# Seven norms of a transformer kernel: three of eight scaled input tiles made by GpSimd instead of VectorE

## Chip, cores and metric

One core of a Trainium2 chip runs the whole program. The metric is the device time of one execution in microseconds (us); of several runs the median is given. Engines: TensorE (PE in the rows, PEld its weight loads), VectorE (DVE), ScalarE (ACT), GpSimd (POOL) and SyncE (SP).

## What is computed

A sequence of 512 tokens, 1024 wide, goes through four layers. Layers 0 and 1 (`first_block`) each have a mixer and an MLP with a LayerNorm behind each; the input of the next matmul is the normed value scaled and shifted by a modulation of a condition vector:

```python
def layer_norm(x, g, b):
    mu = jnp.mean(xf, axis=-1, keepdims=True)
    var = jnp.mean(jnp.square(xf - mu), axis=-1, keepdims=True)
    return (xf - mu) * lax.rsqrt(var + LN_EPS) * g + b
...
x = layer_norm(ALPHA * x + gate * y, ln_g[layer, 0], ln_b[layer, 0])
u = x * (1.0 + scale) + shift          # input of the next matmuls
```

The two hybrid layers (`hybrid_layer`) have RMS norms, once before the mixer and once before the gated feed-forward:

```python
h = rms_norm_2(x, norm_mix) * (1 + sc_m) + sh_m
...
h = rms_norm_2(x, norm_ffn) * (1 + sc_f) + sh_f
```

All is float32.

## The kernel before

Activations lie transposed: 8 tiles of 128 features by 512 tokens each. `X` ("residual") is the residual stream, `H` ("hidden") 32 tiles of work space, `M` ("mixer_out") eight more, `TMP` ("tmp") two, `COL` ("columns") and `GAINS` small columns with one number per partition.

Each float32 matmul is done as three matmuls on rounded parts: a weight panel is split into a high part (ScalarE, line 2024) and a low part (VectorE, line 1275), an input tile likewise into `UHI` ("in_high") and `ULO` ("in_low"), and TensorE multiplies high x high, high x low and low x high. Weight panels stream in by SyncE's DMA queue through a ring of 4; three split panels are kept. `prepare(ahead(...))` places the splitting in each engine's instruction list, always the next panels, and each waits until an older panel has been used.

The work of each engine is an instruction list written out by hand, in program order, with semaphores between the lists: an event name (`mark`, `at`) stands for a semaphore and its value.

A norm, around the change, goes like this. TensorE forms the mean of squares in a bank. ScalarE makes the root (the reciprocal square root) of it, by Ln (line 2066) and Exp (line 2069), and marks it `ln_r` or `rms_r`. VectorE then runs `norm_split` (line 1420): for tile k a scaled tile, `X[k] * gain[k] * root`, written to `H[16 + k]` (line 1429); ScalarE adds the shift and rounds, which gives `UHI[k]` (line 2129, `norm_high`); VectorE forms the low half, `H[16 + k] + shift - UHI[k]`, in `ULO[k]` (line 1424, `tile_low`). VectorE's order is scaled 0, scaled 1, low 0, scaled 2, low 1, and so on, scaled 7, low 6, low 7. TensorE meanwhile runs filler matmuls (`busy`, line 625).

There are seven such norms: `("ln", 0)`, `("ln", 1)`, `("ln", 2)` in the first block (called norm 0, 1 and 2), and `("mix", l)` and `("ffn", l)` for l = 0, 1 in the hybrid layers. They start at about 244.6, 607.0, 952.4, 1324.4, 1695.5, 2062.7 and 2428.6 us (norm 0, 1, 2, mix 0, ffn 0, mix 1, ffn 1). The norm behind the last MLP of the first block and the final one have no such split.

Behind six of them TensorE runs `gemm_pair` (lines 697 to 699): two panels at once on two banks, the second two tiles behind the first, so that a tile brings three matmuls for tiles 0 and 1 and six from tile 2 on; it waits for `norm_out` of each tile. Behind norm 1 it runs a single `gemm` (lines 654 to 656), with three matmuls per tile, and then `gemm_tok` (lines 715 to 717).

In the LayerNorms `layer_norm` (line 1383) first centres the eight tiles of X (line 1392), then makes the columns `LNG` (gain) and `LNS` (shift, lines 1396 to 1399, marked `ln_shift`), and then waits for the root. In mix 0 the tiles of X are finished by line 1413 (`ln_x`). In the others of the hybrid layers they are finished by the residual's additions (line 1336, `x_new`).

GpSimd's list is short: `gpsimd_program` stores rows of the forget gate to memory (line 2630) and loads 16 rows broadcast over the partitions (line 2635), each from the fifth on behind a wait on the attention.

Of the kernel before, what the change touches and what calls it, by code (L numbers as in the profile page):

```python
# [9 lines left out]
KT = D // P  # L10
# [18 lines left out]
L2 = 2  # L29
FF2 = 2816  # L30
FF2_T = FF2 // P
HALF = 16
# [274 lines left out]
class Ledger:  # L307
# [11 lines left out]
    def step(self, name, by=1):  # L319

        sem = self.sem(name)
        self.value[name] += by
        return sem, by

    def mark(self, name, *event, by=1):

        sem = self.sem(name)
        self.value[name] += by
        self.also(name, *event)
        return sem, by  # L330
# [6 lines left out]
    def last(self, name):  # L337

        return self.sem(name), self.value[name]

    def at(self, *event):

        if not self.table:
            return self.sem("unknown"), 1
        name, value = self.table[event]
        return self.sem(name), value


def build(nc, io, table):
    ev = Ledger(nc, table)  # L350
    at, mark, step, last = ev.at, ev.mark, ev.step, ev.last
    v, s, g, pe, sp = nc.vector, nc.scalar, nc.gpsimd, nc.tensor, nc.sync
# [6 lines left out]
    def sb(name, shape, dt=F32):  # L359
        return nc.alloc_sbuf_tensor(name, shape, dt)  # L360
# [5 lines left out]
    X = sb("residual", [P, KT, T])  # L366
# [5 lines left out]
    H = sb("hidden", [P, 32, T])  # L372
# [32 lines left out]
    R = TMP[:, 0, 0:T]  # L405
# [5 lines left out]
    ln_root = lambda i: M[:, 7, :] if i in (0, 2) else R  # L411
    LNG, LNS, RB = (COL[:, 88 + 8 * z:96 + 8 * z] for z in range(3))
# [9 lines left out]
    mix = lambda k: M[:, k, :]  # L422
    u_split = lambda k: (UHI[:, k, :], ULO[:, k, :])
    h_split = lambda k: (HSPLIT[:, 0, k, :], HSPLIT[:, 1, k, :])
    STAGE = 16
    landed = [nc.alloc_semaphore(f"panel_landed_{k}") for k in range(RING)]
    stage_mod = lambda n: MODS[:, 24 * n:24 * n + 24]

# [56 lines left out]
    mix_gain = lambda l: GAINS[:, 16 * l:16 * l + 8]  # L485
    ffn_gain = lambda l: GAINS[:, 16 * l + 8:16 * l + 16]
# [781 lines left out]
    def vector_program():  # L1268
# [114 lines left out]
        def layer_norm(i, gcol_, bcol, mod):  # L1383
# [20 lines left out]
            if mod is not None:  # L1404
                norm_split(("ln", i), lambda k: LNG[:, k:k + 1], lambda k: LNS[:, k:k + 1], ln_root(i))
# [14 lines left out]
        def norm_split(event, gain, shift, root, ready=None):  # L1420

            def tile_low(k):
                v.wait_ge(*at("norm_high", *event, k))
                v.scalar_tensor_tensor(ULO[:, k, :], H[:, STAGE + k, :], shift(k), UHI[:, k, :].bitcast(F32), ALU.add,  # L1424
                                       ALU.subtract).then_inc(*mark("vector_norm", "norm_out", *event, k))
            for k in range(KT):
                if ready is not None:
                    v.wait_ge(*at(*ready, k))
                v.scalar_tensor_tensor(H[:, STAGE + k, :], X[:, k, :], gain(k), root, ALU.mult, ALU.mult).then_inc(
                    *mark("vector_norm", "norm_scaled", *event, k))  # L1430
                if k:
                    tile_low(k - 1)
            tile_low(KT - 1)

        def rms_norm(event, gain, shift):
            v.wait_ge(*at("rms_r", *event))
            norm_split(event, lambda k: gain[:, k:k + 1], lambda k: shift[:, k:k + 1], R,
                       ("ln_x", 3) if event == ("mix", 0) else None)

        def input_low(k, src, high, event):  # L1440
            v.wait_ge(*at(*high))
            v.tensor_tensor(ULO[:, k, :], src, UHI[:, k, :].bitcast(F32), ALU.subtract).then_inc(
                *mark("vector_norm", *event))
# [543 lines left out]
        for n in range(4):  # L1987
            for k in (2 * n, 2 * n + 1):
                prepare(ada_panels[k + 8] + 1)
                v.wait_ge(*at("x", n))  # L1990
                v.wait_ge(*last("modulations"))
                v.tensor_scalar(H[:, STAGE + k, :], X[:, k, :], MODS[:, 8 + k:9 + k], MODS[:, k:k + 1], ALU.mult,
                                ALU.add).then_inc(*mark("vector_start", "u_stage", k))
            prepare(PANELS[("xr", n)][0] + 1)
            for k in (2 * n, 2 * n + 1):
                input_low(k, H[:, STAGE + k, :], ("u_high", k), ("u_low", k))
        even()
# [17 lines left out]
    def scalar_program():  # L2015
# [31 lines left out]
        def input_high(k, src, ready, event):  # L2047
            s.wait_ge(*at(*ready))
            s.activation(UHI[:, k, :], src, ACT.Copy).then_inc(*mark("scalar_norm", *event))
# [76 lines left out]
        def norm_high(event, shift):  # L2126
            for k in range(KT):
                s.wait_ge(*at("norm_scaled", *event, k))
                s.activation(UHI[:, k, :], H[:, STAGE + k, :], ACT.Identity, bias=shift[:, k:k + 1]).then_inc(
                    *mark("scalar_norm", "norm_high", *event, k))  # L2130
# [461 lines left out]
        for n in range(4):  # L2592
            prepare(PANELS[("xr", n)][0] + 1)
            for k in (2 * n, 2 * n + 1):
                input_high(k, H[:, STAGE + k, :], ("u_stage", k), ("u_high", k))
        s.wait_ge(*at("loads"))
# [29 lines left out]


    def gpsimd_program():
        g.wait_ge(*at("forget"))
        g.dma_start(io["forget"], NF).then_inc(*mark("forget_stored", "forget_stored", by=16))  # L2630
        g.wait_ge(*at("forget_stored"))
        for hd in range(FOX_H):
            if hd >= 4:
                g.wait_ge(*at("fox", "max", 8 * ((hd - 4) // 2) + 6 + hd % 2))
            g.dma_start(fox_bias(hd), io["forget"][hd:hd + 1, :].broadcast_to([P, T])).then_inc(
                *mark(f"bias_landed_{hd % 4}", "bias_landed", hd, by=16))


    def sync_program():
# [19 lines left out]
    vector_program()  # L2659
    scalar_program()  # L2660
    gpsimd_program()
    sync_program()
    return ev.made
# [32 lines left out]
```

## Time and profile before

| | us |
|---|---|
| median of 3 runs | 2809.56 |
| lowest and highest run | 2802.15, 2810.24 |
| the profiled execution, its own time | 2805.29 |
| its span | 2803.7 |
| TensorE busy | 2681.7 (96%) |
| VectorE busy | 1626.8 (58%) |
| ScalarE busy | 1153.0 (41%) |
| GpSimd busy | 9.4 (0%) |
| granted TensorE clock, mean | 0.995 |

The span is the time from the first to the last recorded instruction of one profiled execution; all rows come from it. Busy times of TensorE are of pipelined matmuls with modelled ends. "Waits" are idle times of an engine just before an instruction, put down to the instruction that released it. [...]

### The profile page before, as it was taken

Reading aid. Unit: us, or ns where it says so; the run is one execution under the profiler, and the core shown is the slowest. Engines: PE = TensorE matmul, PEld = TensorE weight load, DVE = VectorE, ACT = ScalarE, POOL = GpSimd, SP = SyncE. Lnnn points to the kernel's source line nnn. Section 1 sums busy time; section 2 is a strip of 40 time slices with the busy share of each in tenths; the row PEclk is TensorE's granted clock in tenths of the full one; section 3 lists DMA queues with packets and bytes.
Section 4 is the critical chain, followed back from the end, with each engine's and each line's share of the span. In section 5 each row is a group of like instructions: output and inputs, shape, how many; then the busy total and the mean of one; then the engine's idle time right before and its main releaser. Section 6 shows DMA issues by size and latency. Waiting matters only on the chain.

```text
span 2803.7 us, 41785 instructions
## 1 busy us (share of the span) xinstructions
PE 2681.7 (96%) x17242; PEld 2116.3 (75%) x17242; DVE 1626.8 (58%) x2917; ACT 1153.0 (41%) x2012; POOL 9.4 (0%) x21
## 2 busy tenths in 40 slices
PE   6999999999999999999998899999999988999998
PEld 4777888867666788886886667888878766788886
DVE  6588746573556874667556665444465577533334
ACT  2544324234556442323645553221355466322222
POOL 0000000000000000000000000000000000000000
PEclk9999999999999999999999999999999999999999
DMA  6445555533221365553230013444443200222222
GB/s 256 137 135 181 187 187 177 183 118 107 82 68 54 106 203 201 187 203 130 98 128 17 3 54 121 135 150 143 137 136 107 97 3 3 92 96 98 98 98 83
DMA packets 92093, 336.42 MB, mean 120 GB/s; under 512 B 10480, under 2 KB 10736, under 8 KB 91776
## 3 DMA queue, kind: packets, MB, share of 16 engines
q1 hardware_dynamic: 86800, 315.40, 33.7%
q10 hardware_dynamic: 3792, 14.11, 1.4%
q0 software_dynamic: 1312, 4.23, 0.5%
q8 instruction: 138, 2.26, 0.3%
q14 instruction: 51, 0.42, 0.0%
HBM read 331.57 MB, written 2.13 MB: 119 GB/s over the span
## 4 chain that ended last, share of the span: by engine, by line
PE 46%; ACT 4%; DVE 3%; issue 1%; DVEq 0%; ACTq 0%
PE bank L654 12%; PE bank L655 12%; PE bank L656 12%; PE bank L936 1%; ACT probs L2269 1%; PE bank L921 1%; PE bank L907 1%; PE bank L1008 1%; PE bank L697 0%; PE bank L699 0%; PE bank L698 0%; PE bank L1170 0%; PE bank L996 0%; PE bank L1180 0%; PE bank L1118 0%
## 5 line engine op out<-in xcount | busy, mean ns | idle before, releaser
L1275 DVE TENSOR_TENSOR weights_low<-weight_ring,weights_high 128x1024 fp32r<-128x1024 f32 x404 | 493.8, 1224 | 423.2 <-ACT weights_high L2024 423.0
L654 PE MATMUL bank<-in_high,weights_high 128*128 128x512 f32 x1848 | 725.6, 393 | 9.6 <-DVE in_low L1424 3.4
L655 PE MATMUL bank<-in_low,weights_high 128*128 128x512 f32 x1848 | 720.0, 390 | 0.0
L656 PE MATMUL bank<-in_high,weights_low 128*128 128x512 f32 x1848 | 719.9, 390 | 0.0
L2024 ACT ACTIVATE weights_high<-weight_ring 128x1024 fp32r<-128x1024 f32 x404 | 424.5, 1051 | 419.7 <-PE bank L656 302.2
L654 PEld LDWEIGHTS bank<-in_high,weights_high 128*128 128x128 f32 x1848 | 347.2, 188 | 90.7 <-issue 5.4
L656 PEld LDWEIGHTS bank<-in_high,weights_low 128*128 128x128 f32 x1848 | 347.3, 188 | 72.9
L655 PEld LDWEIGHTS bank<-in_low,weights_high 128*128 128x128 f32 x1848 | 347.3, 188 | 71.0 <-issue 0.5
L654 PE MATMUL bank<-hidden_split,weights_high 128*128 128x512 f32 x864 | 336.9, 390 | 0.0
L656 PE MATMUL bank<-hidden_split,weights_low 128*128 128x512 f32 x864 | 336.1, 389 | 0.0
L655 PE MATMUL bank<-hidden_split,weights_high 128*128 128x512 f32 x864 | 336.1, 389 | 0.0
L1284 DVE CUSTOM_DVE_ANT_0 weight_ring<-weight_ring,silu_c,vectors 128x1024 f32<-128x1024 f32 x192 | 244.4, 1278 | 3.7 <-DMA weight_ring<-stream 3.6
L654 PEld LDWEIGHTS bank<-hidden_split,weights_high 128*128 128x128 f32 x864 | 162.2, 188 | 34.2 <-issue 0.5
L655 PEld LDWEIGHTS bank<-hidden_split,weights_high 128*128 128x128 f32 x864 | 162.2, 188 | 34.0 <-issue 0.5
L656 PEld LDWEIGHTS bank<-hidden_split,weights_low 128*128 128x128 f32 x864 | 162.2, 188 | 33.7
L2139 ACT ACTIVATE hidden_split<-tmp 128x512 fp32r<-128x512 f32 x108 | 68.3, 632 | 269.3 <-DVE tmp L1811 200.8
L2038 ACT ACTIVATE tmp<-bank 128x512 f32<-128x512 f32 (+1 forms) x69 | 41.2, 598 | 219.5 <-PE bank L656 219.0
L1447 DVE TENSOR_TENSOR hidden_split<-tmp,hidden_split 128x512 fp32r<-128x512 f32 x108 | 74.8, 692 | 75.4 <-ACT hidden_split L2139 75.4
L1336 DVE SCALAR_TENSOR_TENSOR residual<-bank,modulations,residual 128x512 f32<-128x512 f32 x64 | 48.0, 750 | 118.7 <-PE bank L656 118.7
L2269 ACT ACTIVATE probs<-probs,columns 128x256 f32<-128x256 f32 (+4 forms) x144 | 73.7, 513 | 102.1 <-DVE columns L1618 100.3
L2038 ACT ACTIVATE tmp<-bank,vectors 128x512 f32<-128x512 f32 (+1 forms) x65 | 44.7, 687 | 129.0 <-PE bank L656 125.8
L1811 DVE TENSOR_TENSOR tmp<-bank,tmp 128x512 f32<-128x512 f32 x44 | 30.4, 692 | 113.6 <-PE bank L656 113.6
(385 smaller groups left out, 3334.9 us busy)
## 6 DMA issues: line engine op xcount, KB each, us to landing
weight_ring<-stream SPq DMA_DIRECT2D x597, 512.0 KB, 3.4
mixer_out<-cmp ACTq DMA_DIRECT2D x6, 1024.0 KB, 5.3
hidden<-forget_rows POOLq DMA_DIRECT2D x16, 256.0 KB, 3.6
residual<-x ACTq DMA_DIRECT2D x4, 512.0 KB, 12.4
mixer_out<-cmp SPq DMA_DIRECT2D x2, 1024.0 KB, 6.3
out<-mixer_out ACTq DMA_DIRECT2D x4, 512.0 KB, 2.7
constants<-consts ACTq DMA_DIRECT2D x1, 1821.5 KB, 20.5
silu_c<-c ACTq DMA_DIRECT2D x2, 512.0 KB, 4.2
```

Source lines behind the costliest of these rows:

```text
L654: pe.matmul(bank[:, :], WHI[:, z, cols], high, start=(k == 0), stop=False)
L655: pe.matmul(bank[:, :], WHI[:, z, cols], low, start=False, stop=False)
L656: ins = pe.matmul(bank[:, :], WLO[:, z, cols], high, start=False, stop=(k == ktiles - 1))
L1275: v.tensor_tensor(WLO[:, z, :], ring[:, n % RING, :], WHI[:, z, :].bitcast(F32), ALU.subtract).then_inc(*mark("weights_low", "low", n))
L1284: v.tensor_tensor_reduce(w, w, SC[:, :], 1.0, vec1("ada_b", col, col + 1), ALU.mult, ALU.add, MODS[:, col:col + 1]).then_inc(*mark("modula ...
L1336: v.scalar_tensor_tensor(X[:, m, :], B_of(key)[:, :], gcol_[:, m:m + 1], X[:, m, :], ALU.mult, ALU.add).then_inc(*mark("residual", "evicte ...
L1447: v.tensor_tensor(HSPLIT[:, 1, at_, :], tmp, HSPLIT[:, 0, at_, :].bitcast(F32), ALU.subtract).then_inc(*mark("vector_mlp", *event))
L1811: v.tensor_tensor(tmp, B_of(("gup", l, j))[:, :], tmp, ALU.mult).then_inc(*mark("vector_mlp", "evicted", ("gup", l, j)))
L2024: s.activation(WHI[:, i % NSPLIT, :], ring[:, n % RING, :], ACT.Copy).then_inc(*mark("weights_high", "high", n))
L2038: s.activation(dst, view(B_of(key)[:, :]), func, **kw).then_inc(*mark("scalar_evict", "evicted", key))
L2139: s.activation(HSPLIT[:, 0, at_, :], tmp, ACT.Copy).then_inc(*mark("scalar_mlp", *event))
L2269: s.activation(p, p, ACT.Exp, bias=nm, scale=-1.0, accum_out=COL[:, c + 2 + z:c + 3 + z]).then_inc(*mark(sem, *name, "exp", i))
```

## The change

VectorE's `norm_split` makes scaled tiles 0 to 4 only. GpSimd makes tiles 5, 6 and 7 in two operations each: X times the gain column, as soon as the tile of X and the gain are there, and, once the root is there, that times the root, in place in `H[16 + k]`. It marks the same event as VectorE did, so ScalarE's `norm_high` waits for it. All eight low halves stay with VectorE. GpSimd's list gets norms 0 and 1 ahead of the forget store, norm 2 behind the bias loads, and then the four norms of the hybrid layers.

```diff
+    POOL_TILES = 5
...
             for k in range(KT):
-                if ready is not None:
-                    v.wait_ge(*at(*ready, k))
-                v.scalar_tensor_tensor(H[:, STAGE + k, :], X[:, k, :], gain(k), root, ALU.mult, ALU.mult).then_inc(
-                    *mark("vector_norm", "norm_scaled", *event, k))
+                if k < POOL_TILES:
+                    if ready is not None:
+                        v.wait_ge(*at(*ready, k))
+                    v.scalar_tensor_tensor(H[:, STAGE + k, :], X[:, k, :], gain(k), root, ALU.mult, ALU.mult).then_inc(
+                        *mark("vector_norm", "norm_scaled", *event, k))
                 if k:
                     tile_low(k - 1)
...
     def gpsimd_program():
+
+        def norm_tiles(event, gain, root, centred, ready):
+            for k in range(POOL_TILES, KT):
+                g.wait_ge(*at(*centred(k)))
+                g.tensor_scalar(H[:, STAGE + k, :], X[:, k, :], gain(k), None, ALU.mult).then_inc(*step("gpsimd_norm"))
+            g.wait_ge(*at(*ready))
+            g.wait_ge(*last("gpsimd_norm"))
+            for k in range(POOL_TILES, KT):
+                g.tensor_tensor(H[:, STAGE + k, :], H[:, STAGE + k, :], root, ALU.mult).then_inc(
+                    *mark("gpsimd_norm", "norm_scaled", *event, k))
+
+        def layer_tiles(i):
+            g.wait_ge(*at("ln_shift", i))
+            norm_tiles(("ln", i), lambda k: LNG[:, k:k + 1], ln_root(i), lambda k: ("ln_centre", i, k), ("ln_r", i))
+
+        layer_tiles(0)
+        layer_tiles(1)
         g.wait_ge(*at("forget"))
...
+        layer_tiles(2)
+        for l in range(L2):
+            g.wait_ge(*at("gains", l, 1))
+            norm_tiles(("mix", l), lambda k: mix_gain(l)[:, k:k + 1], R,
+                       lambda k: ("x_new", "ffn", l - 1, HALF, KT - 1) if l else ("ln_x", 3, k), ("rms_r", "mix", l))
+            g.wait_ge(*at("gains", l, 4))
+            norm_tiles(("ffn", l), lambda k: ffn_gain(l)[:, k:k + 1], R, lambda k: ("x_new", "hyb", l, KT - 1), ("rms_r", "ffn", l))
```

## Rows read from the trace of the kernel before

**Rows 1.** The page: busy time of each engine, and the chain that ended last.
```profile
PE 2681.7 (96%) x17242; PEld 2116.3 (75%) x17242; DVE 1626.8 (58%) x2917; ACT 1153.0 (41%) x2012; POOL 9.4 (0%) x21
...
PE 46%; ACT 4%; DVE 3%; issue 1%; DVEq 0%; ACTq 0%
```
**Rows 2.** TensorE's waits: line waited for, us in total, times, longest us.
```profile
PE bank L697 <- DVE in_low L1424: 8.9, 18, 1.0
...
PE bank L654 <- DVE in_low L1424: 3.4, 7, 1.3
```
**Rows 3.** VectorE's timeline, norm ffn 0: start us, us, engine line op, [idle before].
```profile
1695.50 1.42 DVE L1429 SCALAR_TENSOR_TENSOR hidden<-residual,gains_of_layer,tmp 128x512 f32<-128x512 f32 x2 [3.39 <-ACT tmp L2069]
1697.04 0.75 DVE L1424 SCALAR_TENSOR_TENSOR in_low<-hidden,modulations,in_high 128x512 fp32r<-128x512 f32 x1
...
1701.02 0.75 DVE L1424 SCALAR_TENSOR_TENSOR in_low<-hidden,modulations,in_high 128x512 fp32r<-128x512 f32 x1
1701.68 0.75 DVE L1429 SCALAR_TENSOR_TENSOR hidden<-residual,gains_of_layer,tmp 128x512 f32<-128x512 f32 x1
...
1706.83 1.23 DVE L1275 TENSOR_TENSOR weights_low<-weight_ring,weights_high 128x1024 fp32r<-128x1024 f32 x1 [0.20 <-ACT weights_high L2024]
```
**Rows 4.** TensorE's timeline, the same norm: the first matmul of each tile's three.
```profile
1697.93 0.47 PE L697 MATMUL bank<-in_high,weights_high 128*128 128x512 f32 x1 [0.76 <-DVE in_low L1424]
...
1699.17 0.50 PE L697 MATMUL bank<-in_high,weights_high 128*128 128x512 f32 x1 [0.30 <-DVE in_low L1424]
...
1700.49 0.50 PE L697 MATMUL bank<-in_high,weights_high 128*128 128x512 f32 x1 [0.36 <-DVE in_low L1424]
...
1701.99 0.40 PE L697 MATMUL bank<-in_high,weights_high 128*128 128x512 f32 x1
...
1706.11 0.39 PE L697 MATMUL bank<-in_high,weights_high 128*128 128x512 f32 x1
...
1707.47 0.39 PE L697 MATMUL bank<-in_high,weights_high 128*128 128x512 f32 x1
```
**Rows 5.** TensorE's timeline, norm 1: the first and the last tile.
```profile
609.46 0.47 PE L654 MATMUL bank<-in_high,weights_high 128*128 128x512 f32 x1 [1.35 <-DVE in_low L1424]
...
618.20 0.50 PE L654 MATMUL bank<-in_high,weights_high 128*128 128x512 f32 x1
```
**Rows 6.** ScalarE's timeline, norm ffn 0: the root, and the high half of tile 5.
```profile
1694.77 0.63 ACT L2069 ACTIVATE tmp<-tmp 128x512 f32<-128x512 f32 x1
...
1702.46 0.72 ACT L2129 ACTIVATE in_high<-hidden,modulations 128x512 fp32r<-128x512 f32 x1 [0.60 <-DVE hidden L1429]
```
**Rows 7.** GpSimd's timeline: its forget store.
```profile
629.85 0.62 POOL L2630 DMA_DIRECT2D forget_rows<-hidden  x1 [629.41 <-DVE columns L1660]
```
**Rows 8.** Groups of VectorE by line and shape: count | busy us, mean ns | idle before.
```profile
L1275 DVE TENSOR_TENSOR weights_low<-weight_ring,weights_high 128x1024 fp32r<-128x1024 f32 x404 | 493.8, 1224 | 423.2 <-ACT weights_high L2024 423.0
...
L1457 DVE TENSOR_TENSOR tmp<-tmp 128x512 f32<-128x512 f32 x64 | 44.3, 692 | 53.2 <-ACT tmp L2038 53.0
...
L1413 DVE TENSOR_SCALAR residual<-residual,vectors 128x512 f32<-128x512 f32 x8 | 3.3, 487 | 0.0
```
**Rows 9.** VectorE's timeline where norm 0, norm 1 and mix 0 begin.
```profile
244.57 1.42 DVE L1429 SCALAR_TENSOR_TENSOR hidden<-residual,columns,mixer_out 128x512 f32<-128x512 f32 x2 [4.71 <-issue]
...
606.76 0.16 DVE L1400 TENSOR_SCALAR columns<-vectors 128x8 f32<-128x8 f32 x1
606.96 1.41 DVE L1429 SCALAR_TENSOR_TENSOR hidden<-residual,columns,tmp 128x512 f32<-128x512 f32 x2
...
1324.42 1.42 DVE L1429 SCALAR_TENSOR_TENSOR hidden<-residual,gains_of_layer,tmp 128x512 f32<-128x512 f32 x2 [1.80 <-ACT tmp L2069]
```
**Rows 10.** Stretches: A:B, us, busy of PE, PEld, DVE, ACT, POOL (count), granted clock, DMA.
```profile
1507.40:1514.20 6.80, 4.76 (x124) 3.56 (x116) 5.89 (x18) 4.20 (x17) 0.00 (x0) 1.00 0.01 4
1514.20:1521.00 6.80, 6.19 (x86) 4.64 (x88) 5.31 (x18) 3.91 (x16) 0.00 (x0) 0.50 0.01 4
...
1695.50:1701.00 5.50, 4.08 (x14) 2.10 (x13) 5.37 (x8) 2.83 (x4) 0.00 (x0) 1.00 0.01 3
```

## The prediction

> **What bounds the kernel now.** I read the page first, for the share of each engine and the chain: TensorE is busy 2681.7 of 2803.7 us, VectorE 1626.8, and the chain that ended last runs mostly over the weight matmuls [rows 1]. So a microsecond counts only where it makes TensorE wait, and a VectorE microsecond saved elsewhere is worth nothing. Next I read who waits for the line that the norms end in, the low half L1424: TensorE lost 8.9 us in 18 waits at the paired matmuls and 3.4 us in 7 at the single ones [rows 2]. That is 12.3 us for all seven norms. A change over about 8.4 us (0.3%, about what a measurement of this kernel can tell from no change) would need two thirds of it back.
>
> Third, the timelines of one norm on three engines, the first ffn norm, at 1695.5 us; the other five paired norms have the same pattern, to about 0.1 us. VectorE waits 3.39 us for the root, then issues scaled and low operations in turn with starts 0.66 us apart, so one tile each 1.32 us [rows 3]. TensorE starts tiles 0, 1 and 2 at 1697.93, 1699.17 and 1700.49, each after a wait on VectorE, and then waits no more: tile 3 starts at 1701.99 and tile 7 at 1707.47, so a tile on two banks takes 1.37 us, its three matmuls 0.69 on one [rows 4]. The 18 waits are thus these three in each of six norms. VectorE at 1.32 feeds TensorE at 1.37, with no reserve to speak of: tile 3's low half ends at 1701.77 (1701.02 + 0.75) for matmuls at 1701.99. The norm's whole time for TensorE is decided by how early the first three tiles come; whatever holds VectorE by 1 us in them holds TensorE by nearly 1 us to the end.
>
> Fourth, the one norm with single matmuls (index 1, 607 us). There a tile takes TensorE 0.69 us, so it waits on each up to tile 6; the first is at 609.46, the last at 618.20 [rows 5]. VectorE is the bound over the whole norm, and only here are tiles 5 to 7 on the path.
>
> **The change part by part.** *Removed from VectorE:* three scaled operations in each of seven norms, 21 at a step of 0.66 us, 13.9 us in all. In the six paired norms they lie behind tile 2, where TensorE does not wait, so they are worth 0 there; the cover is the 1.37 us of matmuls per tile. VectorE's next work behind a norm is the low half of a panel, already waiting for ScalarE's high half (0.20 us idle before it in [rows 3]), which waits for a panel to be used: finishing the norm earlier brings it no earlier. In norm 1, tiles 5, 6 and 7 could go at ScalarE's 0.72 us [rows 6] in place of 1.32: 3 x 0.60 = 1.8 us gained, if GpSimd is in time.
>
> *Added on GpSimd:* per norm three multiplications by the gain (one tensor input) and three by the root (two). The trace has no such operation; GpSimd is busy 9.4 us in all, with 16 bias loads, one store and four tiny fills [rows 1]. Bounds for the product with the root, 128x512 with two inputs: 0.69 us, VectorE's tensor_tensor of that size, and 1.22, its tensor_tensor of twice the size [rows 8]. I take 1.22, because a norm gets no shorter by erring low and the engine has never been seen doing such work here. For the multiplication by the gain: 0.49 us (VectorE's one-input operation) to 1.22; I take 0.69. [...]
>
> *Is GpSimd in time?* In the ffn norm its products would end 1.22, 2.44 and 3.66 us behind the root at 1695.4, by 1699.1 (by about 1701 if each first waits for a VectorE operation); ScalarE turns to tile 5 at 1702.46 [rows 6]. VectorE idles 3.39 us ahead of the root in the ffn norms and in mix 1, 4.71 in norm 0, 1.80 in mix 0 [rows 3, 9]: there the gain multiplications hide (3 x 0.69 = 2.1 us; in mix 0 they can start behind the last additions to X, about 0.8 us ahead of the pause). In norms 1 and 2 the shift columns come only 0.2 us before VectorE's own first tile (606.76 against 606.96 in [rows 9]), so the gain multiplications run beside VectorE. Even there six operations end within 5.8 us, before tile 5 is due. GpSimd's queue: norms 0 and 1 are placed ahead of the forget store at 629.85 [rows 7], which they clear by 13 us; norm 2 stands behind the bias loads, which are long over by then. Nothing queued is late.
>
> *Unknown: what GpSimd's operations do to VectorE beside them.* Every VectorE operation of the norm reads two tiles from SBUF (hidden and in_high, residual and root) and writes a third [rows 3]. From below the cost is 0: the engines run side by side. From above it is the whole duration of each GpSimd operation: while one runs, the other stands. I take the upper end, as the operands of both are the same kind and the same tiles. [...]
>
> Then, per norm, taking turns: three products of 1.22 put 3.66 us between VectorE's first operations: behind scaled 0, behind scaled 1, behind low 0. TensorE's tile 2 comes 3.66 us later, and later tiles keep their distance. Norms 0, mix 0, mix 1, ffn 0, ffn 1: 5 x 3.66 = 18.3 us. Norm 2 adds 3 x 0.69 = 2.1 us of gain multiplications: 5.7. Norm 1: 5.7 less the 1.8 gained: 3.9. Sum 18.3 + 5.7 + 3.9 = 28 us slower. With the low prices (0.69 and 0.49): 5 x 2.07 + 3.54 + 1.74 = 15.6.
>
> *The clock.* [...] Such a stretch costs up to 3.4 us of matmul time; I allow half of it for each norm, 12 us, and put it into the upper end, not the sum, since TensorE would be waiting for VectorE in part of it.
>
> **The rivals.** *A, taking turns* (the forecast): +28 us on the profiled execution's 2805.3 us (span 2803.7 and 1.6 around it), so 2833. The median of the runs, 2809.6, lies 4.3 us above that execution and their lowest, 2802.2, 3 below; I leave the sum where the profile puts it. For it: both engines read the same two kinds of tiles out of the same memory in the same 5 us, and VectorE has no pause in which three products would fit before tile 3. Own range 2818 to 2848. Chance 0.63.
> *B, side by side* (not slower): VectorE's 0.75 us stay 0.75 beside GpSimd. Nothing changes in six norms, norm 1 gains 1.8: 2803.5. It decides as long as GpSimd's product stays under about 3.4 us (tile 7's matmuls start at 1707.47 in [rows 4]; its low and high half take 0.75 and 0.72, so the third product must end by about 1705.8, 10.4 us behind the root). For it: the tiles are late in order. [...] Chance 0.22.
> *C, VectorE keeps its turn:* its operations overlap by 0.08 us, so GpSimd may get in only where VectorE pauses. The first long pause would be behind low 3, at 1701.77, as low 4 now waits for ScalarE. Then the three products run to about 1706.9 in turn with low 4 and 5, low 6 ends about 1707.7 instead of in time for 1706.1: 1.7 us per paired norm, with norm 1 about level: +10, 2815. Chance 0.12.
> *D, clearly faster:* only the 3.4 us at single matmuls can shrink by moving late tiles [rows 2], so 8.4 us is beyond the mechanism; 0.03 is left for what I do not see.
>
> **Numbers.** Forecast 2833. The range 2804 to 2848 reaches from B's edge to A with dear products and some clock lost. Slower by over 0.3%: A and two thirds of C, 0.71; faster 0.04 (D, noise on B); same 0.25.
>
> **What would show it.** Under A: scaled and low operations of tiles 0 to 2 keep near 0.75 us in length or grow to about 2, but their starts spread by 1.2 us, TensorE's waits on L1424 grow from 12.3 to about 40 us, and L1429 counts 35 instead of 56. Under B: starts 0.66 us apart as before, with GpSimd's rows beside them. Under C: GpSimd's first product starts or ends about 6 us behind the root. The forecast is wrong if tile 2's matmuls start at the same distance from the root as now (5.1 us), or if GpSimd's product takes over 2 us, when A would near 2850.

## The result and the profile after

The changed kernel takes 2837.8 us, the median of 4 runs (2835.6 to 2839.1), against 2806.8 of the kernel before (4 runs, 2802.2 to 2810.2). The ratio is 1.0112 with a 95% interval of 1.0097 to 1.0126: 31 us slower. The profiled execution took 2839.1 us (span 2837.6), 33.8 above the one of before.

VectorE first, the same norm as in [rows 3] (ffn 0), timeline of the changed kernel (start, length, engine, line; the scaled tiles are now line 1431, the low halves 1425):

```profile
1711.08 1.75 DVE L1431 SCALAR_TENSOR_TENSOR hidden<-residual,gains_of_layer,tmp 128x512 f32<-128x512 f32 x2 [3.39 <-ACT tmp L2071]
1712.96 1.54 DVE L1425 SCALAR_TENSOR_TENSOR in_low<-hidden,modulations,in_high 128x512 fp32r<-128x512 f32 x1
1714.43 1.77 DVE L1431 SCALAR_TENSOR_TENSOR hidden<-residual,gains_of_layer,tmp 128x512 f32<-128x512 f32 x1
1716.12 1.75 DVE L1425 SCALAR_TENSOR_TENSOR in_low<-hidden,modulations,in_high 128x512 fp32r<-128x512 f32 x1
1717.80 0.74 DVE L1431 SCALAR_TENSOR_TENSOR hidden<-residual,gains_of_layer,tmp 128x512 f32<-128x512 f32 x1
```

GpSimd beside it (timeline; the three operations of the first line are those with the gain, of the second those with the root). Over all norms a product with the root shows as 1.3 to 1.8 us, most often as 1.7:

```profile
1707.87 4.64 POOL L2635 TENSOR_SCALAR hidden<-residual,gains_of_layer 128x512 f32<-128x512 f32 x3 [362.39 <-DVE residual L1337]
1712.65 4.67 POOL L2639 TENSOR_TENSOR hidden<-hidden,tmp 128x512 f32<-128x512 f32 x3
```

Three VectorE operations are 0.8 to 1.0 us longer than 0.75 us, and they are the three beside GpSimd's three products (1712.65 to 1717.3). The moment GpSimd is done, VectorE is back at 0.74 us. The first pair, 1.75 us in place of 1.42, runs beside the tail of the third gain product (1710.94 to 1712.51).

TensorE in the same norm. Tiles 0, 1, 2 and 7 start 3.67, 6.95, 8.39 and 16.01 us behind the root (at 1710.98), where [rows 4] has 2.53, 3.77, 5.09 and 12.07 behind 1695.40:

```profile
1714.65 0.47 PE L698 MATMUL bank<-in_high,weights_high 128*128 128x512 f32 x1 [1.89 <-DVE in_low L1425]
...
1717.93 0.79 PE L698 MATMUL bank<-in_high,weights_high 128*128 128x512 f32 x1 [2.34 <-DVE in_low L1425]
1718.52 0.63 PE L699 MATMUL bank<-in_low,weights_high 128*128 128x512 f32 x1
...
1719.37 0.67 PE L698 MATMUL bank<-in_high,weights_high 128*128 128x512 f32 x1
...
1726.99 0.39 PE L698 MATMUL bank<-in_high,weights_high 128*128 128x512 f32 x1
```

From tile 1 until 1720.9 its matmuls take 0.63 us in place of 0.40 and come 0.43 us apart in place of 0.23. The stretches say why (columns as in [rows 10], the clock is the third number from the end, 1.00 being full speed):

```profile
1711.00:1717.50 6.50, 2.69 (x9) 1.24 (x7) 6.29 (x5) 2.11 (x3) 6.17 (x4) 1.00 0.01 3
1717.50:1721.00 3.50, 3.07 (x7) 2.31 (x8) 3.37 (x6) 1.83 (x3) 0.00 (x0) 0.51 0.00 0
```

TensorE stood for more than half of 6.5 us, and then had 0.51 of its clock, that is, nearly all of the second stretch at half speed (0.50 over 1717.60 to 1720.90). Each of the seven norms has such a half-speed stretch in this profile, 3.4 us long in three and 6.8 in four, 37.5 us together; the kernel before has none in a norm.

Over the program, TensorE's waits on the low halves grew from the 12.3 us of [rows 2] to 29.9:

```profile
PE bank L698 <- DVE in_low L1425: 24.2, 16, 2.5
...
PE bank L655 <- DVE in_low L1425: 5.7, 5, 2.4
```

And VectorE, with 21 operations fewer, is busier: 1636.5 us against 1626.8, GpSimd 78.3 against 9.4:

```profile
PE 2696.7 (95%) x17242; PEld 2128.3 (75%) x17242; DVE 1636.5 (58%) x2896; ACT 1151.1 (41%) x2012; POOL 78.3 (3%) x63
```

Where do the 33.8 us of this profile arise? Fillers aside, both traces hold the same 17096 matmuls in the same order, so the start of each can be set against its start before. Take a norm as the stretch from 2.5 us ahead of VectorE's first scaled tile to 22 us behind it, in the time of the kernel before. TensorE then loses 5.1, 1.7, 4.0, 4.6, 3.9, 6.0 and 4.1 us in the seven norms, 29.4 in all: it stands 16.5 us longer, and is busy 12.9 us longer with the same matmuls. Ahead of the first norm it is 2.8 us late already, and the parts between and behind the norms make the rest.

### The profile page after: what moved, and what is told of

It is laid out like the page before. It is cut to its first block, busy times and chain, and to the rows that moved or that the text cites. A ratio compares the mean times of both kernels' runs of the same rounds, so it can differ in the third digit from the quotient of the medians.

```text
span 2837.6 us, 41822 instructions
## 1 busy us (share of the span) xinstructions
PE 2696.7 (95%) x17242; PEld 2128.3 (75%) x17242; DVE 1636.5 (58%) x2896; ACT 1151.1 (41%) x2012; POOL 78.3 (3%) x63
## 3 DMA queue, kind: packets, MB, share of 16 engines
q1 hardware_dynamic: 86800, 315.40, 33.8%
## 4 chain that ended last, share of the span: by engine, by line
PE 45%; DVE 4%; ACT 4%; issue 1%; DVEq 0%; ACTq 0%
PE bank L655 12%; PE bank L656 12%; PE bank L657 12%; ACT probs L2271 1%; PE bank L937 1%; PE bank L922 1%; PE bank L698 1%; PE bank L1009 1%; PE bank L908 1%; DVE hidden L1431 0%; PE bank L699 0%; PE bank L700 0%; DVE in_low L1425 0%; PE bank L1171 0%; PE bank L997 0%
## 6 DMA issues: line engine op xcount, KB each, us to landing
residual<-x ACTq DMA_DIRECT2D x4, 512.0 KB, 12.3
```

## The experiments

The theories. *Turns*: a GpSimd operation that reads SBUF keeps a VectorE operation with two SBUF inputs waiting, whatever data they work on. *Late tiles*: the cost comes from waiting for GpSimd's scaled tiles. Beside turns, *the clock*: part of the cost is TensorE's half-speed stretches that the longer stops set off.

**1. GpSimd's operations without anyone waiting for them.** VectorE makes all eight tiles as before; GpSimd works on constants and a scratch tile at the same moments.

```diff
+    SCR = sb("scratch", [P, T])
...
+        def extra(which):
+            for _ in range(3):
+                if ev.value.get("gpsimd_extra"):
+                    g.wait_ge(*last("gpsimd_extra"))
+                if which == 0:
+                    ins = g.tensor_scalar(SCR[:, :], const("cos"), vec1("final", 0, 1), None, ALU.mult)
+                else:
+                    ins = g.tensor_tensor(SCR[:, :], SCR[:, :], const("sin"), ALU.mult)
+                ins.then_inc(*step("gpsimd_extra"))
+
+        def norm_tiles(centred, ready):
+            g.wait_ge(*at(*centred))
+            extra(0)
+            g.wait_ge(*at(*ready))
+            extra(1)
```

> The kernel before, all eight scaled tiles by VectorE, plus six GpSimd operations in each of the seven norms at the times of the change (three one-input products, then three two-input products behind the root). They read constants and write a scratch tile that nobody reads, so no engine waits for them. Taking turns: each GpSimd operation that runs beside VectorE makes one VectorE operation about 1.0 us longer (as 0.75 became 1.75 us), so this costs at least what the change did, about 30 us (25 to 40). Rival, late tiles (the cost comes from waiting for GpSimd's scaled tiles): within 3 us of before, and VectorE's operations keep 0.75 us.

Measured: ratio 1.0108 (1.0093 to 1.0123), 30 us slower (28 by the medians), as much as the change. VectorE's timeline of ffn 0 in this kernel, with GpSimd's products at 1711.62 to 1716.30:

```profile
1711.72 1.77 DVE L1430 SCALAR_TENSOR_TENSOR hidden<-residual,gains_of_layer,tmp 128x512 f32<-128x512 f32 x1
1713.41 1.75 DVE L1425 SCALAR_TENSOR_TENSOR in_low<-hidden,modulations,in_high 128x512 fp32r<-128x512 f32 x1
...
1716.76 0.74 DVE L1425 SCALAR_TENSOR_TENSOR in_low<-hidden,modulations,in_high 128x512 fp32r<-128x512 f32 x1
```

No engine waits for a GpSimd result here, so late tiles falls as the cause. The cost is the mere presence of GpSimd's operations. It is also as large with VectorE's 21 scaled operations back in place: in the six paired norms TensorE loses 28.0 us here and 27.7 in the changed kernel, so taking them away brought nothing there.

**2. GpSimd writing only.** As 1, with six fills of the scratch tile in place of each three operations.

```diff
-            for _ in range(3):
+            for _ in range(6):
...
-                    ins = g.tensor_scalar(SCR[:, :], const("cos"), vec1("final", 0, 1), None, ALU.mult)
+                    ins = g.memset(SCR[:, :], 0.0)
...
-                    ins = g.tensor_tensor(SCR[:, :], SCR[:, :], const("sin"), ALU.mult)
+                    ins = g.memset(SCR[:, :], 0.0)
```

> The kernel before plus twelve GpSimd fills of the scratch tile (128x512) in each norm, six ahead of the root and six behind: operations that write SBUF and read nothing. If the two engines take turns only over reading, VectorE's operations keep 0.75 us and the time is within 3 us of before. If they take turns over any SBUF access, VectorE's operations beside the fills grow and the time is 15 us or more above before. Late tiles: within 3 us of before.

Measured: 1.0003 (0.9993 to 1.0012), no difference. The groups of GpSimd by line (us busy, mean ns), and VectorE's timeline where six of the fills run from 1696.30 to 1699.74:

```profile
L2638 POOL MEMSET scratch<- 128x512 f32 x42 | 22.0, 525 | 4.0 <-ACT mixer_out L2070 1.3
```
```profile
1697.58 0.75 DVE L1425 SCALAR_TENSOR_TENSOR in_low<-hidden,modulations,in_high 128x512 fp32r<-128x512 f32 x1
```

VectorE keeps 0.74 to 0.75 us beside the fills. GpSimd's fills, which only write, did not hold it; the products of run 1, which also read, held it to 1.75 to 1.77.

**3. VectorE reading one tile from SBUF and one from PSUM.** As 1, but three two-input products beside the centring of X (X minus a bank) in the four LayerNorms, and nothing in the norms.

```diff
+        def extra(i):
+            g.wait_ge(*(at("ln_mean", i) if i else at("ln_mean", i, KT - 1)))
+            for _ in range(3):
...
+                g.tensor_tensor(SCR[:, :], SCR[:, :] if _ else const("cos"), const("sin"), ALU.mult).then_inc(*step("gpsimd_extra"))
```

> The kernel before plus three GpSimd two-input products on constants and a scratch tile beside the centring of X in each of the four LayerNorms, where VectorE reads one tile from SBUF and one from PSUM. If turns are taken only against VectorE operations with two SBUF inputs, the centring keeps 0.68 us and the time stays within 3 us of before. If GpSimd's reading holds every VectorE operation, some centrings grow to about 1.7 us and the four norms are later by up to 3 us each, 12 us in all.

Measured: 1.0001 (0.9992 to 1.001). VectorE's and GpSimd's timelines at norm 1:

```profile
602.55 1.88 DVE L1393 TENSOR_TENSOR residual<-residual,bank 128x512 f32<-128x512 f32 x3 [2.25 <-issue]
```
```profile
602.90 2.63 POOL L2636 TENSOR_TENSOR scratch<-scratch,constants 128x512 f32<-128x512 f32 x2
```

The centrings keep 0.68 us each (three in 1.88, overlapped; 0.67 to 0.69 for all 32 of the four norms), and GpSimd's products go at 1.3 us in place of 1.7. With one operand in PSUM the two engines ran side by side. Runs 1 to 3 together: operations of VectorE with two SBUF inputs were held (0.75 us became 1.75), and that only beside GpSimd operations that read SBUF. The hold is not the length that the profile shows for the GpSimd operation: VectorE lost 1.0 us to a product that shows as 1.3 us where it need not wait (run 6), and 0.43 to a gain operation of at least 1.56 us (run 5).

**4. The products with the root later.**

```diff
             g.wait_ge(*last("gpsimd_norm"))
+            g.wait_ge(*at("norm_out", *event, 2))
             for k in range(POOL_TILES, KT):
```

> The changed kernel, with GpSimd's three products with the root started only when VectorE has the low half of tile 2. Taking turns: the first three tiles are no longer held by products, and the holds fall where tiles 5 to 7 give VectorE 2 us back, so about 12 us above before (8 to 20) instead of 31. Rival, late tiles: tiles 5 to 7 come about 5 us later still, so clearly more than 31 us above before.

Measured: 1.0054 (1.0037 to 1.0071), 15 us slower than before and half of the change's 31, although tiles 5 to 7 come later. VectorE is held as much as in the changed kernel, but in the low halves of tiles 3 to 7, five in 6.50 us (3.61 in the changed kernel), behind GpSimd's products at 1707.93:

```profile
1708.34 6.50 DVE L1425 SCALAR_TENSOR_TENSOR in_low<-hidden,modulations,in_high 128x512 fp32r<-128x512 f32 x5
```

TensorE's waits on the low halves are 19.2 us here, and it loses 14.1 us in the norms. Two things make up the saving. With the shorter stops only norms 1 and 2 keep a half-speed stretch, 10.2 us together in place of 37.5. And the holds themselves count for less: in the five paired norms without such a stretch TensorE loses 1.9 us each, where it loses 3.2 when the holds fall on the first tiles at full clock (run 10). So when VectorE is held counts, and not only for how long in total.

**5. The gain on GpSimd, the root on VectorE.**

```diff
+                else:
+                    v.wait_ge(*at("norm_gained", *event, k))
+                    v.tensor_tensor(H[:, STAGE + k, :], H[:, STAGE + k, :], root, ALU.mult).then_inc(
+                        *mark("vector_norm", "norm_scaled", *event, k))
...
-            for k in range(POOL_TILES, KT):
-                g.tensor_tensor(H[:, STAGE + k, :], H[:, STAGE + k, :], root, ALU.mult).then_inc(
-                    *mark("gpsimd_norm", "norm_scaled", *event, k))
```

> The changed kernel with GpSimd doing only the three one-input products with the gain; VectorE does the products with the root for tiles 5 to 7 (16 operations a norm, as before). Taking turns: only the gain products that run on behind the root cost, three in norms 1 and 2, one or two in the others: 9 to 14 us above before. Rival, only the two-input products collide (my sum let the gain products hide in five norms and took 0.69 us for each): under 6 us above before.

Measured: 1.0016 (1.0006 to 1.0025), 4 to 5 us (1.7 to 7), below what I expected of turns and inside the rival's number. But the trace shows that gain products do hold VectorE, only for 0.43 us each (norm 1, VectorE's timeline; 0.74 without a hold):

```profile
611.10 1.17 DVE L1425 SCALAR_TENSOR_TENSOR in_low<-hidden,columns,in_high 128x512 fp32r<-128x512 f32 x1
```

I had priced the one-input operation's hold at the product's 1.0 us. In this profile, 6.4 us above the one of before, TensorE loses 2.3 us in the norms and the rest elsewhere. So of the 31 us some 2 to 5 are the gain's; the rest needs the products.

**6. Only tile 7 on GpSimd.**

```diff
-    POOL_TILES = 5
+    POOL_TILES = 7
```

> The changed kernel with only tile 7 made by GpSimd. Taking turns, one two-input product per norm behind the root holds VectorE 1.0 us, the gain product 0.4 in norms 1 and 2 and nothing elsewhere, less 0.6 gained in norm 1: about 7 us above before, and no half-speed stretch if one shorter stop does not tip the clock. If cost went with the number of tiles alone, clock included, it would be a third of 31, 10 us. Late tiles: 0, since tile 7 alone is in time by far.

Measured: 1.0032 (1.0019 to 1.0045), 9 us (5 to 13). Seven holds of 1.03 us (ffn 0: the two first scaled operations take 2.45 us in place of 1.42) give 7.2. The interval takes in 7 and 10, so the time does not tell a third of everything from the holds alone. The trace does: ffn 0, mix 1 and ffn 1 cost TensorE 1.0 us each, just the hold, and norm 1 0.4. The expectation of no half-speed stretch was wrong: norm 0, norm 2 and mix 0 have one of 3.4 us, and cost 1.95, 1.95 and 1.7. Late tiles' 0 is excluded again. VectorE's and GpSimd's timelines in ffn 0:

```profile
1701.79 2.45 DVE L1431 SCALAR_TENSOR_TENSOR hidden<-residual,gains_of_layer,tmp 128x512 f32<-128x512 f32 x2 [3.39 <-ACT tmp L2071]
```
```profile
1701.77 1.26 POOL L2639 TENSOR_TENSOR hidden<-hidden,tmp 128x512 f32<-128x512 f32 x1 [1.63 <-ACT tmp L2071]
```

The single product is 1.26 us long and holds VectorE 1.03. Where three follow one another, starts of held VectorE operations are 1.69 us apart (1714.43 and 1716.12 in the changed kernel), VectorE's own step of 0.66 and the hold of 1.03. The 1.7 us that the profile shows for the later products take in that VectorE operation; they are no price of the product.

**7. and 8. The change again, and with fillers in TensorE's stops.** The changed kernel once more, unedited, beside one with more filler matmuls (the diff shows the mix pair; the up and the gate pairs are edited likewise):

> The changed kernel as it is, beside the two below on one chip: 1.0112 of before again, within its interval (1.0097 to 1.0126), and a half-speed stretch of TensorE's clock in each of the seven norms.

```diff
-        def gemm_pair(keys, x, ready, between=lambda k: None, idle=5):
+        def gemm_pair(keys, x, ready, between=lambda k: None, idle=5, fill={}):
...
                 between(k)
+                busy(banks[1], fill.get(k, 0))
...
-            gemm_pair(ropes[0:2], u_split, lambda k: ("norm_out", "mix", l, k))
+            gemm_pair(ropes[0:2], u_split, lambda k: ("norm_out", "mix", l, k), idle=8, fill=({1: 3, 2: 4}, {1: 6, 2: 3})[l])
```

> The changed kernel with more filler matmuls (128x384, about 0.33 us each) where TensorE stands in the six paired norms: ahead of tile 0 (8, 10 or 12 in place of 5 or 10) and between tiles 0 and 2 (3 to 9, on the second bank, which is not yet in use). VectorE's holds stay. If the granted clock costs its own part (my reading of the trace: about 10 of the 31 us), the half-speed stretches of these norms go and the time falls by 5 to 10 us against the changed kernel, to 21 to 26 us above before. If the clock costs nothing beside the waits, the time stays within 3 us of the changed kernel.

Measured: the change again 1.0099 (1.0085 to 1.0112), with a half-speed stretch in each of the seven norms as expected; with fillers 1.0093 (1.0077 to 1.0109). Inconclusive: the six paired norms had lost their half-speed stretches, but each filler is two recorded matmuls, 0.67 us and not the 0.33 that I had taken from a row counting both. TensorE's own queue of fillers had become the wait (in ffn 0 twelve recorded matmuls, 4.03 us, stand between tiles 0 and 1, and tile 1 starts behind them without a wait), so the run tells nothing of the clock's price.

**9. and 10. Fillers that fit.** The same with 6 to 11 ahead of tile 0 and 1 to 4 behind it, beside the changed kernel:

```diff
-            gemm_pair(ropes[0:2], u_split, lambda k: ("norm_out", "mix", l, k), idle=8, fill=({1: 3, 2: 4}, {1: 6, 2: 3})[l])
+            gemm_pair(ropes[0:2], u_split, lambda k: ("norm_out", "mix", l, k), idle=6, fill=({1: 1, 2: 2}, {1: 3, 2: 1})[l])
```

> The changed kernel as it is, beside the one below: 28 to 31 us above before.

> The changed kernel with fillers that fit the stops. In the run before, each filler was two recorded matmuls (0.67 us and not 0.33), so they overran the stops and held tiles 0 and 1 back themselves. Now 6, 7, 8 or 11 ahead of tile 0 and 1 to 4 between tiles 0 and 2. VectorE's holds stay. If the clock costs its own part, the half-speed stretches of the six paired norms go, and the time falls 5 to 10 us below the changed kernel beside it. If it costs nothing beside the waits, it stays within 3 us of it.

Measured: the changed kernel 2838.1 us (5 runs, 2832.8 to 2842.2; ratio 1.0107, 1.0091 to 1.0122), with fitting fillers 2830.6 (5 runs, 2828.6 to 2834.2; ratio 1.0087, 1.0074 to 1.01). The medians are 7.5 us apart; the intervals still touch, so that size is a likely one and not a sharp one. TensorE's tile 1 in ffn 0, behind fillers from 1711.68 to 1713.78, and the stretch around it:

```profile
1714.19 0.50 PE L699 MATMUL bank<-in_high,weights_high 128*128 128x512 f32 x1 [0.41 <-DVE in_low L1426]
```
```profile
1712.00:1719.00 7.00, 6.23 (x24) 4.14 (x23) 6.87 (x10) 4.29 (x7) 1.58 (x1) 1.00 0.00 0
```

Tile 1 starts as late behind VectorE as in the changed kernel (3.28 us behind tile 0 in both), but the clock stays at 1.00. Only norm 1, which got no fillers, keeps its half-speed stretch. Matmul by matmul, as above, TensorE loses 19.0 us in the six paired norms here, and 27.7, 28.5 and 26.9 in the three profiles of the changed kernel (the one taken beside this run has its stretch in six of the seven norms; norm 2 has none). So VectorE's holds at the first tiles cost about 19 us there, and the slower clock that the longer stops bring 8 to 9.5 more.

No kernel tried here beats the one before.

## Why the prediction was right

**The sign, the mechanism and the size** held: forecast 2833, measured 2838, rival A (taking turns). Run 1 shows the mechanism apart from everything else, and runs 2 and 3 show its conditions. B (side by side) fell with the first rows of the profile after; C (VectorE keeps its turn) too, since GpSimd's first product ends 3 us behind the root and not 6. D (clearly faster) did not come. Tile 2 starts 8.4 us behind the root and not 5.1, and no product takes 2 us, so neither sign of being wrong is there. That the sum came within 3 us is partly luck: it had the holds too dear and the clock at nothing, as follows.

**What bounds the kernel** held: 21 VectorE operations removed brought nothing in the paired norms (run 1).

**The product's hold was mis-sized.** I took 1.22 us and a hold of the whole of it, 3.66 us a norm. The length was nearly right, 1.3 us where the product need not wait (runs 3 and 6), but it holds VectorE for 1.0: 3.0 a norm. "The whole duration" as the upper end was an assumption that no row showed, and the mis-sized term. The holds in all, with those of the gain, were to cost TensorE 28 us; they cost some 19 in the paired norms (run 10) and, with its stretch, 1.7 in norm 1 (the profile after).

**The gain's price was wrong**, 0.69 us against 1.56, and with it the step that hid it in five norms. Three take 4.64 us and not 2.1, so in ffn 0 the third (it begins at 1710.94) runs past the root at 1710.98. Its hold is only 0.43 us, so the miss cost little: run 5 puts the gain at 2 to 5 us in all, where my sum had 4.1 for norms 1 and 2.

**The clock was placed in the upper end only and belonged in the sum.** The 12 us allowed for it were my estimate from one place in [rows 10], 6.80 us at 0.50 behind 6.80 us in which TensorE is busy 4.76: half of the 3.4 us that such a stretch can cost, in each norm. I kept it out of the sum because TensorE would be waiting in part of it. No row showed what a norm's longer stop does to the clock. In the runs it fell to 0.50 in all seven norms in two profiles of the changed kernel and in six in the third. Run 10 returned 7.5 us by the medians. The clock's 8 to 9.5 us are what the too-dear holds stood in for. TensorE's waits grew by 17.6 us (29.9 less 12.3), not by 28 as the prediction's "about 40" said, and they show less than the holds cost. That fits with slow matmuls filling a part of the time in which TensorE would have stood, but no run shows it apart.

**Is GpSimd in time** was wrong in norms 1 and 2, where the six operations take over 10 us and not 5.8. In both ScalarE waited 0.9 us for the last one, at 624.88 and 972.14. VectorE did not stop for it, and run 1, where nothing waits for GpSimd, cost the same within its interval, so this decided nothing. **Norm 1's** net loss was forecast as 3.9 us. From VectorE's first operation to TensorE's last tile it went from 11.2 us (606.96 to 618.20 in [rows 5, 9]) to 14.7 (614.40 to 629.11), 3.5. Only 1.7 of it reaches the rest of the program: right behind, at 625.91, TensorE in the kernel before waits 1.3 us for a panel's low half, and in the changed kernel it does not. My sum had left that out.

**The sum as measured:** about 19 of holds and 8 to 9.5 of clock in the paired norms, and 1.7 in norm 1, 29.4 in the profile after (31.6 and 28.6 in the two others of the changed kernel), against 31 by the medians. **Left open:** how much of norm 1's 1.7 is its stretch, and why the parts outside the norms differ between profiles (below).

## What to carry to other kernels

Before moving work from VectorE to GpSimd, look at what VectorE does beside it: here operations with two SBUF inputs were held when GpSimd read SBUF (0.75 us became 1.75), those with one operand in PSUM were not (0.67 to 0.69 us), and GpSimd's fills were free (0.74 to 0.75). An idle engine is then no free engine, and 0.66 us taken off VectorE cost it 1.0. And where TensorE waits tile by tile, a hold in the first tiles counted in full (3.2 us for a norm's three products and the gain's tail), the same hold later six tenths (1.9); a stop that grows may bring the slower clock on top, here 8 to 9.5 us for six norms.

## What the runs showed that I had not expected

A VectorE operation of 0.75 us grew by 1.0 us beside a two-input GpSimd product, which shows as 1.3 us where it need not wait, and by only 0.43 beside a one-input one, which shows as 1.56; the hold is not the length that the profile shows, and the longer of the two operations held less.

TensorE's half-speed stretches come and go in parts of the program that no edit touches. The profile of before has one of 3.4 us at 1405 us, the changed one has none there; the changed one has two of 3.4 us in the first 115 us, where the code is the same, and is 2.8 us later than before ahead of the first norm. Outside the norms the three profiles of the changed kernel stand 4.4, -0.4 and 8.2 us above the one of before. One profiled execution can so differ from another by a few microseconds in parts that the change does not touch.
